# Triangular inverse of a gated delta rule: blocks of 32 built packed, with 32x32 products on the array's diagonal tiles

## What is computed

```python
h = rmsnorm(x, even_norm_mix[e])
dn_qkv, dn_a, dn_b, dn_gate, fq, fk, fv = split_cols(h @ even_w_in[e], IN0_SPLITS)
...
g = -exp(A_log) * softplus(a + dt_bias);  beta = sigmoid(b)
decay = where(tri, exp(gdiff), 0)
Lmat = where(strict, beta * (k @ k.T) * decay, 0) + eye(CHUNK)
sol = triangular_solve(Lmat, rhs, lower=True, unit_diagonal=True)
```

## Time and profile before

| | |
|---|---|
| median of 3 runs | 1422.94 us (1422.93 to 1423.54) |
| the profiled execution | 1423.36 us, of which the span of the profile is 1421.7 us |
| PE busy | 1372.3 us, 97% of the span, 6907 matmuls |
| DVE, ACT, POOL busy | 825.6 us (58%), 582.8 us (41%), 132.2 us (9%) |
| mean granted clock of PE | 0.98 |

### The profile page before, as it was taken

How to read it: one execution, slowest core, us unless ns; L and a number is a source line. 1 busy time by engine, 2 the same in 40 slices (tenths; PEclk the granted TensorE clock), 3 DMA queues, 4 the chain that set the end, 5 groups by cost and what they waited for, 6 DMA issues and landing times.

```text
span 1421.7 us, 19333 instructions
## 1 busy us (share of the span) xinstructions
PE 1372.3 (97%) x6907; PEld 1126.2 (79%) x6907; DVE 825.6 (58%) x1243; ACT 582.8 (41%) x807; POOL 132.2 (9%) x141
## 2 busy tenths in 40 slices
PE   7999899999899999999999999999999999999996
PEld 6878879777678888888888777777878888888885
DVE  4786685677475655345655555555655654355543
ACT  5333232355444443223334455554435442233342
POOL 1050040011041100000001100100210000000011
PEclk9899899999999999999999999999999999999998
DMA  8211110124144633343223432233223333433132
GB/s 247 85 42 31 45 30 16 45 60 130 34 128 133 180 83 89 96 118 89 77 74 104 113 88 73 72 90 100 60 81 96 90 94 89 114 93 111 56 93 59
DMA packets 218659, 124.77 MB, mean 88 GB/s; under 512 B 6063, under 2 KB 215450, under 8 KB 218356
## 3 DMA queue, kind: packets, MB, share of 16 engines
q1 hardware_dynamic: 213760, 112.48, 28.1%
q0 software_dynamic: 3664, 11.58, 2.8%
q10 hardware_dynamic: 1188, 0.08, 0.1%
HBM read 119.87 MB, written 9.48 MB: 91 GB/s over the span
## 4 chain that ended last, share of the span: by engine, by line
PE 91%; DVE 5%; ACT 2%; issue 1%; DMA 1%; ACTq 0%; POOL 0%; DVEq 0%; POOLq 0%
PE acc L672 73%; PE R L795 4%; PE acc L1045 3%; PE R L914 2%; PE R L928 2%; PE R L694 1%; PE R L1018 1%; ACT wh L389 1%; PE R L793 1%; PE R L977 1%; DVE cta L1585 1%; DVE wl L393 1%; DMA prow<-in_even_diff_subln 1%; DMA out<-ob 0%; DVE ml L1512 0%
## 5 line engine op out<-in xcount | busy, mean ns | idle before, releaser
L672 PE MATMUL acc<-mh,wh 128*128 128x512 f32 x1120 | 318.8, 405 | 2.6 <-ACT wh L1205 1.7
L672 PE MATMUL acc<-ml,wh 128*128 128x512 f32 x1120 | 312.7, 397 | 3.1 <-DVE ml L1512 3.1
L672 PE MATMUL acc<-mh,wl 128*128 128x512 f32 x1120 | 309.5, 395 | 1.0 <-DVE wl L1594 0.9
L393 DVE TENSOR_TENSOR wl<-raw,wh 128x2048 fp32r<-128x2048 f32 (+1 forms) x103 | 222.1, 2156 | 118.1 <-ACT wh L389 118.1
L389 ACT ACTIVATE wh<-raw 128x2048 fp32r<-128x2048 f32 (+1 forms) x111 | 200.6, 1807 | 134.2 <-PE acc L672 134.2
L672 PEld LDWEIGHTS acc<-ml,wh 128*128 128x128 f32 x1120 | 211.4, 191 | 50.1 <-DVE ml L1512 4.6
L672 PEld LDWEIGHTS acc<-mh,wh 128*128 128x128 f32 x1120 | 206.7, 190 | 53.9 <-issue 10.0
L672 PEld LDWEIGHTS acc<-mh,wl 128*128 128x128 f32 x1120 | 211.0, 190 | 45.7 <-DVE wl L1594 1.3
L538 POOL TENSOR_TENSOR ssum<-ssum,sq 128x512 f32<-128x512 f32 x32 | 49.9, 1561 | 737.2 <-ACT sq L1156 736.5
L2051 DVE SCALAR_TENSOR_TENSOR cta<-cb,pv,cta 128x512 f32<-128x512 f32 x88 | 66.2, 752 | 74.1 <-ACT cta L1451 67.7
L672 PE MATMUL acc<-al,wh 128*128 128x512 f32 x352 | 95.4, 389 | 0.0
(11 more groups left out here) (314 smaller groups left out, 1643.0 us busy)
## 6 DMA issues: line engine op xcount, KB each, us to landing
raw<-in_ffn_w_in SPq DMA_DIRECT2D x88, 512.0 KB, 5.0
raw<-in_ffn_w_out SPq DMA_DIRECT2D x32, 384.0 KB, 4.0
raw<-in_even_w_in SPq DMA_DIRECT2D x23, 512.0 KB, 5.2
raw<-in_ffn_w_out SPq DMA_DIRECT2D x32, 320.0 KB, 3.7
raw<-in_odd_w_qkv SPq DMA_DIRECT2D x16, 512.0 KB, 4.6
rel_bias_extended<-rel_bias_rows POOLq DMA_DIRECT2D x16, 320.0 KB, 3.9
raw<-in_even_w_out SPq DMA_DIRECT2D x8, 512.0 KB, 4.5
raw<-in_odd_w_qkv SPq DMA_DIRECT2D x16, 256.0 KB, 3.1
```

The source lines that it names most:

```text
L393: nc.vector.tensor_tensor(wl[s][:, 0:n], raw[s][:, 0:n], wh[s][:, 0:n].bitcast(F32), ALU.subtract).then_inc(sem(f"w_tail{s}"), 1)
L672: last = nc.tensor.matmul(acc[2 * s + t][:, :], ws[0 if form[0] else 1][:, t, k, :], mov[0 if form[1] else 1][:, k, :], start=form == HEAD ...
```

## The change

**Tables and masks.** Three masks of 32 columns join the constants (`C_I32`, `C_L16`, `C_L32`). The jobs `At` to `X16` leave `_DN`; in their place stand eight packed jobs, each for both heads at once. Packed means: the 32x32 diagonal blocks of N of both heads and four token blocks, 32 in all, lie as four quarters of partitions by eight blocks of 32 columns, 128x256 in all.

**PE.** `tiles(name, *products)` replaces `step` up to width 32. It issues, for each of eight column blocks and each quarter q, one product of 32x32 weights by 32 columns at `tile_position` (32q, 32q):

```diff
+                def tiles(name, *products):
+                    r = job(ph, name, 0)
+                    for at, a, b in products:
+                        for n in range(8):
+                            for q in quarter:
+                                last = nc.tensor.matmul(r[q, at + 32 * n:at + 32 * n + 32], small[a][q, 32 * n:32 * n + 32],
+                                                        small[b][q, 32 * n:32 * n + 32], start=True, stop=True,
+                                                        tile_position=(q.start, q.start))
+                    done(last, ph, name, 0)
+
+                two, few = 2 if p == 0 else 1, g[5]
+                g = ((4, 4, 3, 3, 2, 2), (2, 2, 2, 2, 1, 1))[p]
+                pe.wait_ge(sem("small_U0"), p + 1)
+                tiles("c2", (0, "At", "A"), (2 * P, "A", "At"))
+                give(fill, g[0])
+                step(few, "ktok", "kh", None)
+                read(pe, ph, "c2", 0)
+                tiles("c4", (0, "A2t", "A2"), (2 * P, "A2", "A2t"))
+                tiles("cU1", (0, "A2", "U"))
+                give(fill, g[1])
+                read(pe, ph, "c4", 0)
+                tiles("c8", (0, "A4t", "A4"))
+                read(pe, ph, "cU1", 0)
+                tiles("cU2", (0, "A4", "U"))
+                give(fill, g[2])
...
+                tiles("cU3", (0, "A8", "U"))
...
+                tiles("cY", (0, "E", "U"))
...
+                tiles("cX", (0, "T", "Y"))
+                give(fill, g[5])
-                step(two, "At", "A", None, need=[("A_E", 4 * p + 1)])
-                step(two, "A2", "At", "A", ["At"])
-                step(two, "A2t", "A", "At")
...
-                step(two, "U3", "A8", "U", ["U2", "A8"])
-                last = "U3"
-                for w, e, g in (("16", "E32", (1, two, 1)), ("32", "E64", (two, 1, two)), ("64", "E128", (1, two, 1))):
+                last = None
+                for w, e, g in (("32", "E64", (two, 1, two)), ("64", "E128", (1, two, 1))):
```

**DVE** takes qh (out of `rq`) ahead of N's decay, packs N while it applies the decay, masks and transposes it itself (a transpose within 32x32 blocks), and unpacks at `cX`:

```diff
+                    for i in range(4):
+                        V.tensor_tensor(packed(small["N"], h, i), diagonal(e["N"], i), diagonal(e["decN"], i), ALU.mult)\
+                            .then_inc(sem("small_N"), 1)
+                dve.wait_ge(sem("small_N"), 8 * p + 8)
+                own(V.tensor_tensor(eight(small["A"]), eight(small["N"]), each_eight(C_L16), ALU.mult), "small_A", p + 1)
+                own(V.transpose(small["At"], small["A"]), "small_At", p + 1)
+                V.tensor_tensor(eight(small["U"]), each_eight(C_I32), eight(small["At"]), ALU.subtract)\
+                    .then_inc(sem("small_U0"), 1)
+                V.tensor_tensor(eight(small["E"]), eight(small["N"]), each_eight(C_L32), ALU.mult)\
+                    .then_inc(sem("small_E"), 1)
```

**The gate columns** are made feature-major first: `ab_features` moves the unsplit x (`xs`, 512 tokens) through 32 columns of weights, scaled by the norm's gain on DVE, in four column groups of the array, and `ab_tokens` adds the four groups and turns them with a 128x8 selector, two groups of projections later:

```diff
+                for a in range(KD // 4):
+                    for g in range(4):
+                        k = 4 * a + g
+                        last = nc.tensor.matmul(r[32 * g:32 * g + 32, :], abw[:, k, :], xs[:, k, :],
+                                                start=(a == 0), stop=(a == KD // 4 - 1), tile_position=(0, 32 * g))
...
-                    for k in range(KD):
-                        nc.tensor.matmul(r[:, b * 16:b * 16 + 16], mh[:, k, t], abx[:, k, :],
-                                         start=(k == 0), stop=False)
-                        last = nc.tensor.matmul(r[:, b * 16:b * 16 + 8], ml[:, k, t], abx[:, k, 0:8],
-                                                start=False, stop=(k == KD - 1))
+                    last = nc.tensor.matmul(r[:, b * 8:b * 8 + 8], abs_[:, b * P:(b + 1) * P], pick[:, :],
+                                            start=True, stop=True)
```

More of the change, by code:

```diff
@@ L64 @@
 C_COS, C_SIN, C_MASK = 8 * P, 8 * P + S, 8 * P + 2 * S
-C_WIDTH = 8 * P + 3 * S
+C_I32, C_L16, C_L32 = [8 * P + 3 * S + 32 * n for n in range(3)]
+C_WIDTH = 8 * P + 3 * S + 96
 def constants():
@@ L286, in build, with eight, each_eight, diagonal @@
         mix.close()
+        abs_ = d[1]["U"]
+        small = {}
+        for n, where, at in (("A", d[0]["A"], 0), ("At", d[0]["A"], 1), ("N", d[1]["A"], 0), ("E", d[1]["A"], 1),
+                             ("A2", d[0]["A2"], 0), ("A2t", d[0]["A2"], 1), ("A4", d[0]["A2t"], 0),
+                             ("A4t", d[0]["A2t"], 1), ("A8", d[1]["A2"], 0), ("T", d[1]["A2"], 1), ("U", d[1]["A2t"], 0),
+                             ("Y", d[1]["A2t"], 1)):
+            small[n] = where[:, at * 2 * P:(at + 1) * 2 * P]
+        quarter = [slice(32 * n, 32 * n + 32) for n in range(4)]
+        def eight(t):
+            return t.rearrange("p (g n) -> p g n", n=32)
+        def each_eight(c):
+            return cst[:, c:c + 32].unsqueeze(1).broadcast_to([P, 8, 32])
+        def diagonal(t, i):
+            return blk(t)[quarter[i], :, quarter[i]]
+        def packed(t, h, i):
+            return eight(t)[quarter[i], 4 * h:4 * h + 4, :]
         mixer = ExitStack()
@@ L543, in _ @@
             pool.wait_ge(sem("x_kept"), 16)
+            full(pool, "ab", "abT", 0)
             pool.wait_ge(sem("m_tail"), KD)
@@ L1082, in _ @@
             run(first, 4)
+            ab_features()
+            run(first, 2)
             ab_tokens()
@@ L1298, in dn_pair, with small_out @@
                     next(evac, 0)
[L1299 to L1303, removed]
+                def small_out(name, dst, pieces=0):
+                    r = full(act, ph, name, 0)
+                    free(A(dst, r[:, 0:dst.shape[1]], ACT.Copy), ph, name, 0)
+                    for _ in range(pieces):
+                        next(evac, 0)
+                small_out("c2", d[0]["A2"], 1)
+                small_out("c4", d[0]["A2t"], 2)
+                small_out("c8", small["A8"])
+                small_out("cY", small["Y"], 0 if p else 1)
                 copy_out("T32", "T", 0 if p else 2)
@@ L1747, in dn_pair @@
                                                 op0=ALU.mult, op1=ALU.mult), ph, f"rq{h}", 0)
+                for h in (0, 1):
+                    e = d[h]
+                    dve.wait_ge(sem(f"eN{h}"), p + 1)
+                    for i in range(4):
[8 more added lines that the diff above has]
+                    .then_inc(sem("small_E"), 1)
+                for h in (0, 1):
+                    e = d[h]
+                    own(V.tensor_tensor(e["N"], e["N"], e["decN"], ALU.mult), f"N{h}", p + 1)
+                piece("N")
                 piece("qh")
@@ L1764, in dn_pair @@
                 piece("ktok")
-                for h in (0, 1):
-                    e = d[h]
-                    read(dve, ph, f"At{h}", 0)
-                    V.tensor_tensor(blk(e["U"]), rows(ident), blk(e["At"]), ALU.subtract).then_inc(sem(f"U0{h}"), 1)
-                piece("At")
                 def copy(name, dst):
```

115 lines of the change are left out of this document (70 added, 45 removed), and 2 rows, old and new, of the table _DN.

## The result

The changed kernel takes **1415.97 us** (median of 5 runs, 1414.05 to 1416.82) against 1422.94 before: a ratio of 0.9950, 95% interval 0.9938 to 0.9961. It is faster by 0.5%, or 7.0 us, where the prediction had 20. The likeliest case there was 1398 to 1408 us and the wide range 1394 to 1416; the time lies at the upper edge of the second. The profiled execution took 1416.82 us over a span of 1415.1.

A forecast was written before the change was run, and what follows sets the result against it. PE bounds the kernel, busy 97% of the span. Removed steps -39.3, packed products +25.4, gate columns -7.8 and waits +1.7 sum to -20.0 us: 1403 from 1422.94, likeliest 1398 to 1408, wide range 1394 to 1416.

The forecast's parts named there:

- The likeliest case: Packed products in the pairs cost 13 to 22 ns an instruction, giving 1398 to 1408 us; chance 0.42.
- Everything behind the pairs is PE's stream too and shifts whole: Code after the pairs: the sum of -20.0 us is carried whole to the end.
- Packed products: In the pairs: 1280 added instructions at 18 ns, 23.0 us, plus 2.4 of edges, together +25.4 us.
- rival (C): Pairs: tiles at 7 to 12 ns, chain of DVE and ACT binds; net -24 to -29, 1394 to 1399 us; chance 0.17.
- Rival (A): Packed products in the pairs: tiles do not overlap, 27 ns an instruction, net -10.9, 1412 us; chance 0.22.
- The wait of `c8`: In the pairs, PE waits for ACT's copy of `c4`: 2.2 us in the first, 0 to 1 in the second.
- that of the first transposes of width 32: Behind `cX`, PE waits for DVE's eight unpacking passes: 0.9 and 1.5 us.
- qh's: In the DeltaNet, PE's wait of 2.5 us for qh, where DVE is reordered, would go.
- Gate columns: Ahead of the pairs: 12.0 us removed, 3.8 added, sum -8.2; 0.4 lost to DVE, so -7.8 us.
- the clock would stay at 1.00: Sign: from the gate columns to the change of pairs, PE's clock stays at its upper level.
- rival (D): Packed stretches bring the lower clock, 2 to 5 us a spell, once or twice a pair: 1408 to 1420; chance 0.05.
- the spell at the change of pairs: Low clock there stays, some 15 us earlier; prediction wrong if it grows or goes, up to 7 us either way.

The follow-up runs named there:

- the two spacers: Only unused tile line2 lengthened: 40 to 64 columns in the changed kernel, 1405.44 us; 40 to 48 in the kernel before, 1432.01 us.
- the packed part by itself, with the address repaired: The changed kernel with the gate features as before and line2 at 72 columns, so ah starts at 147072: 1414.66 us, ratio 0.9955 to the kernel before.
- the longer spacer: The changed kernel with its unused tile line2 lengthened from 40 to 64 columns, nothing else: 1405.44 us, ratio 0.9883 to the kernel before.
- the gate part: The kernel before with only the gate features' part of the change, line2 at 96 columns so ah starts at 147072: 1415.21 us, ratio 0.9958.
- the kernel before with its spacer moved: The kernel before with unused tile line2 lengthened from 40 to 48 columns, nothing else: 1432.01 us, ratio 1.0068.
- ACT's and DVE's pieces moved: The changed kernel, line2 at 64; ACT's pieces put behind the copies of c2, c4, c8, DVE's conv pieces behind small updates: 1396.21 us, ratio 0.9828.
- tile by tile: The changed kernel, line2 at 64 columns, with eight packed products on one diagonal tile, then eight on the next, instead of in turn: 1421.10 us, ratio 1.0011.
- ACT alone: The changed kernel, line2 at 64 columns, with only ACT's pieces put behind the copies of c2, c4 and c8: 1402.21 us, ratio 0.9859.
- all three repairs: The changed kernel with line2 at 64 columns, ACT's pieces moved and DVE's conv pieces moved: 1396.21 us, ratio 0.9828 to the kernel before.

## Why the prediction was wrong

**What failed first is not a term but the sentence behind the sum**, "Everything behind the pairs is PE's stream too and shifts whole". It assumed that every instruction that the change leaves alone keeps its duration. The moved tiles made 1440 passes dearer by about 7 ns, some +10 us (shown both ways, by the two spacers). With the spacer set right the kernel takes 1405.4 us, against the 1403 predicted. That the wide range just holds the measured 1416 is luck: its upper end was drawn for dearer products and a lower clock, and the moved tiles stood nowhere in it. That 1405.4 is so near to 1403 is partly luck too: the terms below are off by about 10 us in one direction and by more than that in the other, and the packed part by itself, with the address repaired, is worth 6.4 us (4.0 to 9.0) where its terms sum to 12.6.

**Packed products: mis-sized, in the good direction.** The sum took 18 ns and, with edges, 25.4 us; measured were 9.5 to 10.8 ns, 12 to 14 us for 1280, and some 15 with the edges, which came out near the 0.2 us a stretch taken for them. So the term was about 10 us too high, though inside the bounds of 7 and 58.5 and where rival (C) had them. The scaling from two column tiles to four diagonal ones would have given 7, the trace came near it; the quarter put on top had no row. Rival (A)'s 27 ns is exactly what the products cost when neighbours share a tile (27.0). The Trainium skill, TensorE: Matmul & The Clock Gate, section "Wait — 56ns, not 53.3ns?", puts a floor of about 25 ns on the distance of matmuls; the trace disagrees where neighbours are on different tiles (9.5) and is near it where they are not. The prediction says that the trace of the kernel before neither shows nor denies that floor, because no instruction in it costs less than 58.5 ns. That is a price per instruction, and the floor is on the distance of two starts. The distance could be read there, at the products of the earlier trace rows in a window of 0.05 us (820.70 to 820.75):

```profile
820.71 0.33 PE L1018 MATMUL R<-odd_pT,odd_av 128*64 128x128 f32 x2
```

Two instructions start within 0.05 us. Start by start, the records of these products alternate between 6 or 7 ns and 102 or 103 ns: neighbours on the two column tiles start nearly together. That spoke against (A) before anything was run.

**Waits: one missed.** The wait of `c8` was forecast at 2.2 and 0 to 1 us and measured 2.0 and 2.1; that of the first transposes of width 32 at 0.9 and 1.5, measured 0.87 and 1.6; qh's is gone. Missed was `ktok`: its first bank is the one `c2` was put in, so its transposes wait for ACT's copy of `c2`, 4.6 us for both pairs. The same mechanism as for `c8`, in the same queue, one product earlier; I had followed the operands and not the banks. With the longer spacer, at another pattern of the clock, the same two waits are 7.2 and 5.1 us.

**Gate columns: right.** 1.86 and 0.81 us against 2.5 and 0.9, and no low clock there. By itself the part is worth 6.0 us (3.6 to 8.4) against 7.8. A spell of 3.4 us behind the token sums (61.93) breaks the sign that the clock would stay at 1.00 up to the change of pairs; the gate part need not be its cause, since the kernel before with its spacer moved has one at the same place of its order (71.00).

**The clock: rival (D) had 0.05 and came true in part.** From 50 us to the second pair's end the lower level holds 37.6 us in the profiled execution, against 13.65 before. A us of busy PE at half clock costs half a us, so this is up to 12 us there. It takes back what the cheap products gave. On average it is less: the mean granted clock is 0.977 over the five runs of the changed kernel and 0.980 to 0.982 over the runs of the kernel before beside the experiments, which is worth 4 to 7 us. With ACT's and DVE's pieces moved it is 0.982, no lower than before, and five of the six short spells are gone; at the change of pairs 10 to 17 us stay in every kernel. The prediction named the spell at the change of pairs as a sign of being wrong if it grew: it grew from 13.65 to 17.1 us, which costs under 2 us of the error. What brings a short spell stays open: packed products without a wait had some (tile by tile), and waits of 2 us and more had some and lacked others.

**The rest adds up, but for 2.6 us.** At the first product after the pairs: -20.0 as predicted, -10 for the cheaper products, +6 for `ktok` and the longer `c8`, +2 for issue, up to +12 for the clock, -2.5 for shorter waits for `gc` and `dn_A` (1.9 and 2.3 us before, 0.3 and 1.4 after), together -12.5, where -15.1 was measured; 2.6 us stay unaccounted for. Of these terms only the product's price and the waits in the queues of ACT and DVE were tested by kernels; the clock's share is worked out.

## To carry to other kernels

When a change resizes any tile, work out how far it moves the tiles allocated behind it, and compare the same untouched row (mean ns of one form) in both traces before explaining a difference by the change; here a spacer of 96 bytes was worth more than the change's measured gain. When PE's part of a serial chain shrinks by tens of us, the small copies and updates between its steps must stand ahead of the bulk work in ACT's and DVE's queues, both at once: ACT alone gave some 3 us, not clear of noise, and both together 8. The version with all three repairs, 1396.2 us, is 1.7% faster than the kernel before.

## What the runs showed of the hardware

- A float32r pass of 512 columns over `ah` costs about 7 ns more (2.4 to 2.6 us for 352) when `ah` does not lie a multiple of 256 bytes from where the weights lie; distances with remainders 32, 128 and 160 cost alike (395 or 396 ns against 389), and moving all tiles by 128 bytes costs nothing (1403.26 us). That the distance to the weights counts, and not to another tile ahead of `ah`, is inferred.
- Float32 products of 32x32 by 32 columns on the four diagonal tiles in turn cost 9.5 ns an instruction, on one tile after the other 27.0. On two column tiles of 64, neighbours start 6 or 7 ns apart. Four column groups of 32 with 512 columns overlap wholly: 16 instructions in 1.86 us.
- PE stands for 2.0 us (2.8 in one kernel) in the middle of packed products with nothing to wait for, and goes on some 2.4 us after a packet of instructions (0.02 MB) began to load. That it runs dry of instructions is argued, not shown.
- The clock's lower level came back in pieces of 3.4 us in stretches of otherwise busy PE, often behind waits of 1.6 to 3.8 us. It is no rule: a wait of 3.2 us and stops of 2.0 us had none, and packed products of 27 ns had some without a wait.
